# Half-row level scaling in a chunked linear attention, and a 128-row rope product with a bf16 mask in the latent attention

## The chip, the core and the metric

The kernel runs on one core of a Trainium2 chip. The metric is device time in microseconds, measured over whole executions; the medians below come from separate runs. In the rows, PE is the matrix engine, PEld its weight load, DVE the vector engine, ACT the scalar engine, POOL the GpSimd engine and SP the engine that issues most DMAs.

## What is computed

The kernel computes two transformer blocks on 512 tokens with a model width of 1024: a layer with gated linear attention (4 heads, key width 128, value width 256), a SwiGLU layer, a layer with latent attention (8 heads, 128 plain and 64 rotated key columns), a SwiGLU layer, then a block with a pooling and a convolution branch, and an expert layer with 16384 experts. Only two places matter here.

The linear attention, within one chunk (the reference takes 64 positions, the kernel 128, which is the same sum):

```python
b = jnp.cumsum(gi, axis=-2)
diff = b[:, :, :, None, :] - b[:, :, None, :, :]
decay = jnp.exp(jnp.where(causal, diff, -jnp.inf))
attn = jnp.einsum('bhik,bhjk,bhijk->bhij', qi, ki, decay)
o_intra = jnp.einsum('bhij,bhjv->bhiv', attn, vi)
```

The latent attention, for a block of 128 queries:

```python
s = (jnp.einsum('bqhd,bkhd->bhqk', qn_b, k_nope)
     + jnp.einsum('bqhd,bkd->bhqk', qr_b, k_rope)).astype(jnp.float32) * scale
p = jax.nn.softmax(jnp.where(mask, s, -jnp.inf), axis=-1)
return jnp.einsum('bhqk,bkhd->bqhd', p.astype(v.dtype), v)
```

## The kernel before

Each engine has its own instruction stream, written out by hand; `wait_ge` and `then_inc` on semaphores tie them together. Nothing reorders the work: what stands behind a waiting instruction on its engine waits too. Activations lie with features on the partitions and the 512 tokens along the free dimension. Large weights arrive as 128x1024 blocks in a ring of four buffers; ACT rounds a block to `w_hi`, POOL subtracts to get `w_lo` (L551), and PE makes three products for each pair (`unit`), all recorded at L1626, the line of the helper `mm`.

**The linear attention.** The decayed product of a chunk of 128 positions is built from 7 levels and a diagonal. At level `l` the chunk is cut into blocks of `2s` with `s = 128 >> (l + 1)`; queries in the second half of a block meet keys in its first half, both scaled by `exp(-|b - b_ref|/16)` with the reference position in the middle. An item is one head and one level (or the diagonal), 4 x 8 = 32 items. For an item DVE subtracts the reference (`gate_sums`, L1211), ACT takes the absolute value and the exponential in place (L693, L694, two buffers `g_E`), DVE scales queries and keys (`scaled`, L1219 and L1220, two buffers each), PE multiplies in four chunks of 128 columns into one of four banks of `pa` (`items`), and DVE copies what the level's mask keeps into `g_attn` (`keep`, L1228). DVE's order in turn n is: gate sums of the next item, scaling of item n, mask copy of item n-1. PE does items 0 to 17 in pairs between the projection blocks of `v` and `r`, and items 18 to 31 one after the other behind the twelfth block. Two more blocks of `r` follow on PE, while ACT and DVE scale `g_q` and `g_k` for the state's products, for which PE then waits.

**The latent attention.** 8 heads times 4 query blocks make 32 steps. In step s PE computes the scores of query block `s % 4` against 128, 256, 384 or 512 keys, and after them the transposes of step s-2 (1 to 4 of 128 columns, L1905); once per head it adds the 8 records of the product with `v`. The scores are three products that accumulate in one bank: `m_kn` with `m_qn` (128 rows), `m_kr` with `m_qr` (64 rows: even heads in partitions 0 to 63, odd heads in 64 to 127) and an fp32 product of the identity with the causal mask for the last 128 columns. DVE takes the maximum (L1384) and its negative (L1385), ACT the exponential with its sum (L857), and DVE, in step s+1 behind the maximum of that step, the reciprocal (L1389) and the scaling (L1391), on which the transposes wait. ACT copies the transposes out (L864). The rotated key `m_kr` is made once before that (L1367 to L1369), and ACT waits for it (`kr_done`) before it reads the rotated queries' products into the same buffers (L830).

Of the kernel before, what the change touches and what calls it, by code (L numbers as in the profile page):

```python
# [24 lines left out]
BF16 = mybir.dt.bfloat16  # L25
# [123 lines left out]
def two_blocks(nc, A, out):  # L149
# [59 lines left out]
    g_E = ar("g_E", 56 * K, [2, S])  # L209
    g_qs = ar("g_qs", 60 * K, [2, S])  # L210
    g_ks = ar("g_ks", 64 * K, [2, S])
    g_ln = ar("g_ln", 56 * K, [GH, S])
# [25 lines left out]
    m_v = ar("m_v", 40 * K, [TT, MH * MVD])  # L238
    m_kr = ar("m_kr", 56 * K, [S])
    m_cos = ar("m_cos", 58 * K, [S])  # L240
# [11 lines left out]
    c_hi = at("c_hi", ada_off, [5, S], F32R)  # L252
    m_st = at("m_st", ada_off + 10 * K, [MH * TT, 4])

    ssq = ar("ssq", 0, [DT, S])
# [517 lines left out]
    def act_mla(act, hi):  # L773
# [42 lines left out]
        for t in range(12):  # L816
# [4 lines left out]
            if t < MH:  # L821
                nc.scalar.activation(m_qn[:, t, :], bank, ACT.Copy).then_inc(tile_free, 1)
            else:
                j = t - MH
                act.wait_ge(kr_done, 1)
                if j >= 2:
                    act.wait_ge(qr_done, j - 1)
                dst = (m_sw, m_kraw)[j % 2]
                for q in range(4):
                    nc.scalar.activation(dst[32 * q:32 * q + 32, :], bank[32 * (q ^ 1):32 * (q ^ 1) + 32, :], ACT.Copy)\  # L830
                      .then_inc(sw_done, 1)
# [327 lines left out]
    def dve_gla(dve):  # L1159
# [42 lines left out]
        def gate_sums(e):  # L1202
# [8 lines left out]
            nc.vector.tensor_tensor(E, b, ref, ALU.subtract).then_inc(lv_d, 1)  # L1211

        def scaled(n):

            h, l, e = item_level(n)
            dve.wait_ge(lv_e, e + 1)
            if e >= 2:
                dve.wait_ge(lv_mm, (e - 2) // LEVELS * (LEVELS + 1) + (e - 2) % LEVELS + 1)
            nc.vector.tensor_tensor(g_qs[:, e % 2, :], g_q[:, h, :], g_E[:, e % 2, :], ALU.mult)  # L1219
            nc.vector.tensor_tensor(g_ks[:, e % 2, :], g_k[:, h, :], g_E[:, e % 2, :], ALU.mult).then_inc(lv_q, 1)  # L1220

        def keep(n):
# [3 lines left out]
            if n:  # L1226
                dve.wait_ge(lv_cp, n)
            nc.vector.copy_predicated(g_attn[:, h, :].rearrange("p (c i) -> p c i", c=TT), bc(g_mask[:, l, :], 1, TT),  # L1228
                                      pa[:, n % 4, :].rearrange("p (c i) -> p c i", c=TT)).then_inc(lv_cp, 1)

# [103 lines left out]
    def dve_mla(dve):  # L1334
# [31 lines left out]
        dve.wait_ge(tile_free, T0["mla_qn"])  # L1366
        step(v.tensor_tensor(m_kr[:, :], m_kraw[:, :], m_cos[:, :], ALU.mult))  # L1367
        step(v.tensor_tensor(m_sw[:, :], m_sw[:, :], m_sin[:, :], ALU.mult))
        v.tensor_tensor(m_kr[:, :], m_kr[:, :], m_sw[:, :], ALU.add).then_inc(kr_done, 1)  # L1369
        T = T0["mla_qr"]  # L1370
# [338 lines left out]
    def pe_gla(pe):  # L1709
# [11 lines left out]
        def items(n):  # L1721

            while taken[0] < n:
# [8 lines left out]
                for c in range(TT):  # L1732
                    w = slice(c * GCH, (c + 1) * GCH)
                    kk, qq = (g_ks[:, e % 2, w], g_qs[:, e % 2, w]) if l < LEVELS else (g_k[:, h, w], g_q[:, h, w])
                    last = mm(pa[:, a % 4, w], kk, qq, True, True)
# [103 lines left out]
    def pe_mla(pe):  # L1839
# [46 lines left out]
        pe.wait_ge(qr_done, MH // 2)  # L1886
        pe.wait_ge(kr_done, 1)
        n_it = MH * TT
        for s in range(n_it + 3):
            if s < n_it:  # L1890
# [3 lines left out]
                n, q = P * (qb + 1), slice(qb * P, (qb + 1) * P)  # L1894
                half = slice(ROPE * (h % 2), ROPE * (h % 2 + 1))
                mm(pa[:, s % 3, 0:n], m_qn[:, h, q], m_kn[:, h, 0:n], True, False)
                mm(pa[:, s % 3, 0:n], m_qr[half, h // 2, q], m_kr[half, 0:n], False, False)
                mm(pa[:, s % 3, n - P:n], ident, const("causal_t", P), False, True).then_inc(at_s, 1)
            if 2 <= s < n_it + 2:
# [267 lines left out]
```

## Time and profile before

| | |
|---|---|
| median of 3 runs | 3224.52 us (3216.39 to 3231.88) |
| profiled execution | 3218.98 us, its span 3217.1 us |
| mean granted TensorE clock | 0.983 of full speed |
| PE / DVE / ACT / POOL busy | 96% / 50% / 36% / 55% |
| linear attention, items behind the last projection block | 189.7 to 225.5 us |
| latent attention, score steps | 806.8 to 902 us |

Busy time of PE is the time in which a matmul was in flight, so that it can be near 100% while the array is not at its peak. An fp32 matmul stands as two records, and each streams its columns twice; an fp32r matmul stands as one. The span is cut at the first and last instruction.

### The profile page before, as it was taken

The numbers are of one execution on the slowest core, as the hardware profiler recorded it, in microseconds if no ns is written. First come the engines' busy times: TensorE is split into PE (matmuls) and PEld (weight loads), VectorE is DVE, ScalarE is ACT, GpSimd is POOL, SyncE is SP. The second block draws the span as 40 slices with busy tenths as digits, with TensorE's granted clock in tenths as the row PEclk, the third lists the DMA queues.
The fourth block names the chain that finished last, engine by engine and source line by source line (L and its number), as shares of the span: only waits on it lengthen the run. The fifth ranks groups of instructions, "written<-read, shape, count | busy, mean of one in ns | idle before, by whom it ended". The sixth has DMA issues, their size and how long they took to land.

```text
span 3217.1 us, 44185 instructions
## 1 busy us (share of the span) xinstructions
PE 3085.6 (96%) x14632; PEld 2500.8 (78%) x14632; DVE 1608.6 (50%) x2785; ACT 1151.3 (36%) x1478; POOL 1775.1 (55%) x2040
## 2 busy tenths in 40 slices
PE   5988999998999999997999999999999999999998
PEld 3777788876568888775788888888888888888887
DVE  7873455322435552595316997444421444544443
ACT  4354322226342223433333234555543332333332
POOL 4833677645037766673545665444445666666663
PEclk8989999999999999998999999999999999999999
DMA  7511455522015554221323444555555655556552
GB/s 307 208 35 57 145 200 176 167 77 90 7 61 199 199 172 133 89 84 54 104 92 98 151 147 144 196 187 194 193 198 190 209 192 182 180 195 209 201 190 78
DMA packets 170201, 481.94 MB, mean 150 GB/s; under 512 B 15360, under 2 KB 48896, under 8 KB 168080
## 3 DMA queue, kind: packets, MB, share of 16 engines
q1 hardware_dynamic: 147680, 410.83, 39.1%
q10 hardware_dynamic: 22448, 70.14, 5.6%
q8 instruction: 46, 0.75, 0.1%
q14 instruction: 27, 0.22, 0.0%
HBM read 411.70 MB, written 69.21 MB: 149 GB/s over the span
## 4 chain that ended last, share of the span: by engine, by line
PE 52%; issue 23%; POOL 21%; DVE 2%; ACT 0%; DMA 0%; DVEq 0%; POOLq 0%; SPq 0%; ACTq 0%
PE ps L1626 49%; POOL w_lo L551 21%; PE pa L1626 4%; DVE s_acc L1420 1%; DMA e_g<-expert_act 0%; DVEq L1417 0%; DVE s_pb L1432 0%; DVE s_tmp L1471 0%; DVE mg_lo L1473 0%; ACT mg_hi L921 0%; DVE s_m L1469 0%; DVE x L1125 0%; POOLq L549 0%; POOLq L555 0%; DVE s_gl L1412 0%
## 5 line engine op out<-in xcount | busy, mean ns | idle before, releaser
L551 POOL TENSOR_TENSOR w_lo<-raw,w_hi 128x256 fp32r<-128x256 f32 x2036 | 1774.9, 903 | 1412.6 <-ACT w_hi L569 1411.3
L1626 PE MATMUL ps<-h_hi,w_hi 128*128 128x512 f32 x2392 | 944.8, 395 | 33.4 <-POOL w_lo L551 22.8
L1626 PE MATMUL ps<-h_hi,w_lo 128*128 128x512 f32 x2392 | 934.2, 391 | 0.0
L1626 PE MATMUL ps<-h_lo,w_hi 128*128 128x512 f32 x2392 | 914.5, 390 | 0.0
L569 ACT ACTIVATE w_hi<-raw 128x1024 fp32r<-128x1024 f32 x509 | 538.6, 1060 | 803.9 <-PE ps L1626 685.5
L1626 PEld LDWEIGHTS ps<-h_hi,w_hi 128*128 128x128 f32 x2392 | 450.6, 188 | 133.7 <-POOL w_lo L551 24.5
L1626 PEld LDWEIGHTS ps<-h_hi,w_lo 128*128 128x128 f32 x2392 | 450.6, 188 | 95.5
L1626 PEld LDWEIGHTS ps<-h_lo,w_hi 128*128 128x128 f32 x2392 | 450.4, 188 | 93.0 <-issue 1.7
L1626 PE MATMUL ps<-wa_hi,w_hi 128*128 128x512 f32 x1024 | 398.5, 389 | 0.5 <-DVE x L1590 0.5
L1626 PE MATMUL ps<-wa_hi,w_lo 128*128 128x512 f32 x1024 | 398.4, 389 | 0.0
L1626 PE MATMUL ps<-wa_lo,w_hi 128*128 128x512 f32 x1024 | 398.3, 389 | 0.0
L1072 DVE CUSTOM_DVE_ANT_0 ada<-ada,cvec 128x1024 f32<-128x1024 f32 x144 | 229.3, 1630 | 34.9 <-DMA ada<-in_ada 30.7
L1626 PEld LDWEIGHTS ps<-wa_hi,w_hi 128*128 128x128 f32 x1024 | 192.3, 188 | 40.8 <-DVE x L1590 0.9
L1626 PEld LDWEIGHTS ps<-wa_hi,w_lo 128*128 128x128 f32 x1024 | 192.3, 188 | 39.9
L1626 PEld LDWEIGHTS ps<-wa_lo,w_hi 128*128 128x128 f32 x1024 | 192.3, 188 | 39.8
L1583 DVE TENSOR_TENSOR wa_lo<-e_t,wa_hi 128x512 fp32r<-128x512 f32 x128 | 137.4, 1074 | 153.8 <-ACT wa_hi L1008 153.8
L928 ACT ACTIVATE g_act<-ps 128x512 f32<-128x512 f32 x128 | 76.5, 598 | 348.1 <-PE ps L1626 348.1
L1580 DVE TENSOR_TENSOR e_t<-e_g,e_w 128x512 f32<-128x512 f32 x128 | 110.4, 863 | 168.1 <-DMA e_g<-expert_act 167.3
L1590 DVE SCALAR_TENSOR_TENSOR x<-ps,mod,x 128x512 f32<-128x512 f32 x128 | 95.5, 746 | 158.5 <-PE ps L1626 158.3
L1008 ACT ACTIVATE wa_hi<-e_t 128x512 fp32r<-128x512 f32 x128 | 80.8, 631 | 222.6 <-DVE e_t L1580 222.6
L1555 DVE TENSOR_TENSOR oh_hit<-iota_t,r_key 128x1024 bf16<-128x1024 bf16 x64 | 45.9, 718 | 213.5 <-PE pa L1626 213.1
L988 ACT ACTIVATE w_st<-pa 128x512 f32<-128x512 f32 x128 | 134.7, 1167 | 39.3 <-PE pa L1626 39.3
(315 smaller groups left out, 3104.7 us busy)
## 6 DMA issues: line engine op xcount, KB each, us to landing
ada<-in_ada SPq DMA_DIRECT2D x144, 512.0 KB, 4.4
raw<-in_expert_u SPq DMA_DIRECT2D x128, 512.0 KB, 4.1
raw<-in_expert_v SPq DMA_DIRECT2D x128, 512.0 KB, 4.2
raw<-in_ffn_in SPq DMA_DIRECT2D x88, 512.0 KB, 3.5
expert_act<-g_act ACTq DMA_DIRECT2D x128, 256.0 KB, 4.2
gate_matrix<-w_st ACTq DMA_DIRECT2D x16, 2048.0 KB, 6.9
e_w<-gate_matrix SPq DMA_DIRECT2D x16, 2048.0 KB, 11.4
e_g<-expert_act SPq DMA_DIRECT2D x128, 256.0 KB, 7.5
```

The lines of the kernel that those rows point to most:

```text
L551: last = nc.gpsimd.tensor_tensor(w_lo[:, k, c:c + 256], raw[:, k, c:c + 256], w_hi[:, k, c:c + 256].bitcast(F32), ALU.subtract)
L569: nc.scalar.activation(w_hi[:, k, :], raw[:, k, :], ACT.Copy).then_inc(hi_done, 1)
L928: nc.scalar.activation(g_act[:, k % 2, :], ps[:, (T + k) % RING, :], ACT.Gelu_apprx_tanh)\
L988: nc.scalar.activation(w_st[:, b, :, 4 * q:4 * q + 4].rearrange("p n t -> p t n"), pa[:, q % 4, :].rearrange("p (t n) -> p t n", t=4), ACT ...
L1008: nc.scalar.activation(wa_hi[:, b, k, :], e_t[:, :], ACT.Copy).then_inc(wa_h, 1)
L1072: return nc.vector.tensor_tensor_reduce(out=w, in0=w, in1=cvec[:, :], scale=1.0, scalar=0.0, op0=ALU.mult, op1=ALU.add, accum_out=dst).the ...
L1420: v.scalar_tensor_tensor(out=s_acc[:, t, :], in0=s_gl[:, t, bass.ds(i + 1, S)], scalar=cols[:, bass.ds(i + (COLS["dw_kernel"] + t * CK + 1 ...
L1555: v.tensor_tensor(oh_hit[:, b, :, :, :], column, key1, ALU.is_equal).then_inc(oh_hits, 1)
L1580: v.tensor_tensor(e_t[:, :].rearrange("p (t k) -> p t k", k=WTOK), e_g[:, k % 4, :].rearrange("p (t k) -> p t k", k=WTOK), e_w[:, :, k, :] ...
L1583: v.tensor_tensor(wa_lo[:, b, k, :], e_t[:, :], wa_hi[:, b, k, :].bitcast(F32), ALU.subtract).then_inc(wa_done, 1)
L1590: v.scalar_tensor_tensor(out=x[:, k, :], in0=ps[:, (T + k) % RING, :], scalar=mod[:, GATE[6] + k:GATE[6] + k + 1], in1=x[:, k, :], op0=ALU ...
L1626: return nc.tensor.matmul(out, a, b, start=start, stop=stop_)
```

## The change

In the linear attention the two scaled copies `g_qs` and `g_ks` become one tile `g_kq` with four buffers in place of two: the first half of each block of `2s` columns gets the scaled keys, the second half the scaled queries. PE reads it as both operands. The mask copy of a level reads and writes only the columns of second halves, which are the only ones that its mask can keep; the diagonal is copied in full as before. In the latent attention the rotated key stands in two tiles, each with zeros in the 64 partitions of the other parity, so that the rope product uses all 128 rows with both heads' queries; identity and mask are held in bf16 too. The first loads and the convolution are the same as before.

```diff
-    g_qs = ar("g_qs", 60 * K, [2, S])
-    g_ks = ar("g_ks", 64 * K, [2, S])
+    g_kq = ar("g_kq", 60 * K, [4, S])
...
-    m_kr = ar("m_kr", 56 * K, [S])
+    m_kr = [ar("m_kr0", 56 * K, [S]), at("m_kr1", rstd_off, [S])]
...
-                act.wait_ge(kr_done, 1)
+                act.wait_ge(kr_done, 6)
...
+        def halves(row, l, half):
+
+            s = GCH >> (l + 1)
+            return row.rearrange("p (n w) -> p n w", w=2 * s)[:, :, half * s:(half + 1) * s]
+
         def scaled(n):
 
             h, l, e = item_level(n)
             dve.wait_ge(lv_e, e + 1)
-            if e >= 2:
-                dve.wait_ge(lv_mm, (e - 2) // LEVELS * (LEVELS + 1) + (e - 2) % LEVELS + 1)
-            nc.vector.tensor_tensor(g_qs[:, e % 2, :], g_q[:, h, :], g_E[:, e % 2, :], ALU.mult)
-            nc.vector.tensor_tensor(g_ks[:, e % 2, :], g_k[:, h, :], g_E[:, e % 2, :], ALU.mult).then_inc(lv_q, 1)
+            if e >= 4:
+                dve.wait_ge(lv_mm, (e - 4) // LEVELS * (LEVELS + 1) + (e - 4) % LEVELS + 1)
+            for half, rows in enumerate((g_k, g_q)):
+                last = nc.vector.tensor_tensor(halves(g_kq[:, e % 4, :], l, half), halves(rows[:, h, :], l, half),
+                                               halves(g_E[:, e % 2, :], l, half), ALU.mult)
+            last.then_inc(lv_q, 1)
...
+            s = GCH >> (l + 1)
+            nc.vector.copy_predicated(halves(g_attn[:, h, :], l, 1).rearrange("p (c n) i -> p c n i", c=TT),
+                                      bc(halves(g_mask[:, l, :], l, 1), 1, TT),
+                                      halves(pa[:, n % 4, :], l, 1).rearrange("p (c n) i -> p c n i", c=TT)).then_inc(lv_cp, 1)
...
-                    kk, qq = (g_ks[:, e % 2, w], g_qs[:, e % 2, w]) if l < LEVELS else (g_k[:, h, w], g_q[:, h, w])
+                    kk, qq = (g_kq[:, e % 4, w],) * 2 if l < LEVELS else (g_k[:, h, w], g_q[:, h, w])
...
-        step(v.tensor_tensor(m_kr[:, :], m_kraw[:, :], m_cos[:, :], ALU.mult))
+        step(v.tensor_tensor(m_t[:, :], m_kraw[:, :], m_cos[:, :], ALU.mult))
         step(v.tensor_tensor(m_sw[:, :], m_sw[:, :], m_sin[:, :], ALU.mult))
-        v.tensor_tensor(m_kr[:, :], m_kr[:, :], m_sw[:, :], ALU.add).then_inc(kr_done, 1)
+        for a in range(2):
+            mine, other = slice(ROPE * a, ROPE * (a + 1)), slice(ROPE * (1 - a), ROPE * (2 - a))
+            v.memset(m_kr[a][other, :], 0.0).then_inc(kr_done, 1)
+            v.tensor_tensor(m_kr[a][mine, :], m_t[mine, :], m_sw[mine, :], ALU.add).then_inc(kr_done, 1)
+        v.tensor_copy(ident_b[:, :], ident).then_inc(kr_done, 1)
+        v.tensor_copy(causal_b[:, :], const("causal_t", P)).then_inc(kr_done, 1)
...
-                half = slice(ROPE * (h % 2), ROPE * (h % 2 + 1))
                 mm(pa[:, s % 3, 0:n], m_qn[:, h, q], m_kn[:, h, 0:n], True, False)
-                mm(pa[:, s % 3, 0:n], m_qr[half, h // 2, q], m_kr[half, 0:n], False, False)
-                mm(pa[:, s % 3, n - P:n], ident, const("causal_t", P), False, True).then_inc(at_s, 1)
+                mm(pa[:, s % 3, 0:n], m_qr[:, h // 2, q], m_kr[h % 2][:, 0:n], False, False)
+                mm(pa[:, s % 3, n - P:n], ident_b[:, :], causal_b[:, :], False, True).then_inc(at_s, 1)
```

On DVE, in the level loop (`g_E` are the gate sums, `g_qs` and `g_ks` the scaled copies), before:

```order
L1211 TENSOR_TENSOR g_E<-g_b 128x512
L1219 TENSOR_TENSOR g_qs<-g_q,g_E 128x512
L1220 TENSOR_TENSOR g_ks<-g_k,g_E 128x512
L1228 COPY_PREDICATED g_attn<-g_mask,pa 128x512
L1211 TENSOR_TENSOR g_E<-g_b 128x512
```

And the same engine with the change, two turns (levels 4 and 5; the three sizes are partitions, runs and length of a run):

```order
L1212 TENSOR_TENSOR g_E<-g_b 128x512
L1226 TENSOR_TENSOR g_kq<-g_k,g_E 128x64x4
L1226 TENSOR_TENSOR g_kq<-g_q,g_E 128x64x4
L1241 COPY_PREDICATED g_attn<-g_mask,pa 128x32x8
L1212 TENSOR_TENSOR g_E<-g_b 128x512
L1226 TENSOR_TENSOR g_kq<-g_k,g_E 128x128x2
L1226 TENSOR_TENSOR g_kq<-g_q,g_E 128x128x2
```

The order of a turn is unchanged. Three of its four instructions go from 512 to 256 columns.

On DVE, where the key is rotated, before, with the last steps of the latent norm ahead and the first query tile behind:

```order
L1363 TENSOR_TENSOR c_lo<-m_c,c_hi 128x512 x2
L1367 TENSOR_TENSOR m_kr<-m_kraw,m_cos 128x512
L1368 TENSOR_TENSOR m_sw<-m_sw,m_sin 128x512
L1369 TENSOR_TENSOR m_kr<-m_kr,m_sw 128x512
L1375 TENSOR_TENSOR m_qr<-m_cos,ps 128x512
```

And with the change:

```order
L1381 TENSOR_TENSOR m_t<-m_kraw,m_cos 128x512
L1382 TENSOR_TENSOR m_sw<-m_sw,m_sin 128x512
L1385 MEMSET m_kr_99 64x512
L1386 TENSOR_TENSOR m_kr_99<-m_t,m_sw 64x512
L1385 MEMSET m_kr_100 64x512
L1386 TENSOR_TENSOR m_kr_100<-m_t,m_sw 64x512
L1387 CAST ident_b<-consts 128x128
L1388 CAST causal_b<-consts 128x128
```

One add becomes six instructions, and `kr_done` counts all six. On PE the order of products and transposes is the same as before, with the operands of the diff.

## Rows read from the trace of the kernel before

**Rows 1.** The page, busy time of each engine.

```profile
PE 3085.6 (96%) x14632; PEld 2500.8 (78%) x14632; DVE 1608.6 (50%) x2785; ACT 1151.3 (36%) x1478; POOL 1775.1 (55%) x2040
```

**Rows 2.** Windows: stretch, us, busy of each engine, PEclk, DMA share, GB/s.

```profile
132.10:189.70 57.60, 57.60 (x306) 49.68 (x306) 44.69 (x56) 28.43 (x43) 40.10 (x38) 0.97 0.27 83
189.70:225.50 35.80, 26.23 (x134) 23.36 (x133) 31.85 (x53) 14.48 (x24) 0.00 (x0) 0.71 0.05 15
...
806.80:820.20 13.40, 13.18 (x34) 6.42 (x34) 3.91 (x15) 2.40 (x8) 0.00 (x0) 0.62 0.01 3
820.20:893.00 72.80, 70.63 (x288) 39.36 (x288) 33.35 (x118) 30.19 (x92) 0.00 (x0) 1.00 0.00 1
```

**Rows 3.** Timeline of DVE, one level turn: start, us, line, out<-in.

```profile
210.66 0.68 DVE L1211 TENSOR_TENSOR g_E<-g_b 128x512 f32<-128x512 f32 x1
211.26 0.68 DVE L1219 TENSOR_TENSOR g_qs<-g_q,g_E 128x512 f32<-128x512 f32 x1
211.86 0.69 DVE L1220 TENSOR_TENSOR g_ks<-g_k,g_E 128x512 f32<-128x512 f32 x1
212.47 0.72 DVE L1228 COPY_PREDICATED g_attn<-g_mask,pa 128x512 f32<-128x512 uint32 x1
```

**Rows 4.** Timeline of DVE, first and last mask copy of the exposed turns.

```profile
190.81 0.75 DVE L1228 COPY_PREDICATED g_attn<-g_mask,pa 128x512 f32<-128x512 uint32 x1 [0.66 <-PE pa L1626]
...
224.76 0.73 DVE L1228 COPY_PREDICATED g_attn<-g_mask,pa 128x512 f32<-128x512 uint32 x1 [0.19 <-PE pa L1626]
```

**Rows 5.** Timeline of PE, level products at either granted clock.

```profile
207.87 1.13 PE L1626 MATMUL pa<-g_qs,g_ks 128*128 128x128 f32 x8 [1.02 <-DVE g_ks L1220]
...
219.93 3.86 PE L1626 MATMUL pa<-g_qs,g_ks 128*128 128x128 f32 x16 [1.28 <-DVE g_ks L1220]
```

**Rows 6.** Timeline of PE in attention: start, us, line, out<-in.

```profile
847.60 1.02 PE L1626 MATMUL pa<-m_kn,m_qn 128*128 128x512 f32 x2
848.55 1.12 PE L1626 MATMUL pa<-m_kr,m_qr 64*128 64x512 f32 x2
849.61 0.49 PE L1626 MATMUL pa<-consts 128*128 128x128 f32 x2
849.93 0.38 PE L1905 MATMUL ps<-consts,m_P 128*128 128x128 f32 x2
...
851.59 0.55 PE L1905 MATMUL ps<-consts,m_P 128*128 128x128 f32 x3 [0.23 <-DVE m_P L1391]
```

**Rows 7.** Groups by form, 806 to 902 us: busy, mean ns | idle before.

```profile
L1384 DVE TENSOR_REDUCE m_st<-pa 128x1 f32<-128x512 f32 x8 | 5.5, 692 | 26.4 <-PE pa L1626 26.4
...
L1384 DVE TENSOR_REDUCE m_st<-pa 128x1 f32<-128x256 f32 x8 | 3.4, 425 | 6.6 <-PE pa L1626 6.6
```

**Rows 8.** Timeline of ACT in the turn of rows 3.

```profile
211.38 0.63 ACT L693 ACTIVATE g_E<-g_E 128x512 f32<-128x512 f32 x1 [1.12 <-DVE g_E L1211]
212.04 0.63 ACT L694 ACTIVATE g_E<-g_E 128x512 f32<-128x512 f32 x1
```

**Rows 9.** The page: ACT out of PSUM, output in one run and in strides.

```profile
L928 ACT ACTIVATE g_act<-ps 128x512 f32<-128x512 f32 x128 | 76.5, 598 | 348.1 <-PE ps L1626 348.1
...
L988 ACT ACTIVATE w_st<-pa 128x512 f32<-128x512 f32 x128 | 134.7, 1167 | 39.3 <-PE pa L1626 39.3
```

**Rows 10.** Timeline of DVE, second scaling of the first head.

```profile
129.16 1.21 DVE L1220 TENSOR_TENSOR g_ks<-g_k,g_E 128x512 f32<-128x512 f32 x1
```

**Rows 11.** Timeline of PE around bf16 products of the routing stage.

```profile
2016.28 1.56 PE L1626 MATMUL pa<-oh_gate,oh_key 128*128 128x128 bf16 x24
2017.65 0.47 PE L1626 MATMUL ps<-h_hi,w_hi 128*128 128x512 f32 x1
```

**Rows 12.** Timeline of DVE in attention, scaling of a 512-column tile.

```profile
852.63 0.49 DVE L1391 TENSOR_SCALAR m_P<-m_P,m_st 128x512 f32<-128x512 f32 x1
```

**Rows 13.** Timelines of DVE and ACT around the key rotation.

```profile
760.06 1.11 DVE L1369 TENSOR_TENSOR m_kr<-m_kr,m_sw 128x512 f32<-128x512 f32 x1
...
771.76 2.43 ACT L830 ACTIVATE m_sw<-ps 32x512 f32<-32x512 f32 x4 [2.05 <-PE ps L1626]
```

More of the change, by code:

```diff
@@ L253, in two_blocks @@
     m_st = at("m_st", ada_off + 10 * K, [MH * TT, 4])
+    ident_b = at("ident_b", ada_off + 10 * K + 512, [P], BF16)
+    causal_b = at("causal_b", ada_off + 10 * K + 768, [P], BF16)
     ssq = ar("ssq", 0, [DT, S])
@@ L1227, in keep @@
                 dve.wait_ge(lv_cp, n)
-            nc.vector.copy_predicated(g_attn[:, h, :].rearrange("p (c i) -> p c i", c=TT), bc(g_mask[:, l, :], 1, TT),
-                                      pa[:, n % 4, :].rearrange("p (c i) -> p c i", c=TT)).then_inc(lv_cp, 1)
+            if l == LEVELS:
+                nc.vector.copy_predicated(g_attn[:, h, :].rearrange("p (c i) -> p c i", c=TT), bc(g_mask[:, l, :], 1, TT),
+                                          pa[:, n % 4, :].rearrange("p (c i) -> p c i", c=TT)).then_inc(lv_cp, 1)
+                return
+            s = GCH >> (l + 1)
+            nc.vector.copy_predicated(halves(g_attn[:, h, :], l, 1).rearrange("p (c n) i -> p c n i", c=TT),
+                                      bc(halves(g_mask[:, l, :], l, 1), 1, TT),
+                                      halves(pa[:, n % 4, :], l, 1).rearrange("p (c n) i -> p c n i", c=TT)).then_inc(lv_cp, 1)
         dve.wait_ge(tile_free, T0["gla_v"])
@@ L1886, in pe_mla @@
         pe.wait_ge(qr_done, MH // 2)
-        pe.wait_ge(kr_done, 1)
+        pe.wait_ge(kr_done, 6)
         n_it = MH * TT
```

## The prediction

> **What bounds the kernel now.** I read the page's engine lines first: PE is busy for 96% of the span, the others for at most 55% [rows 1]. So the change pays where PE waits, or where PE's own work gets shorter, and nowhere else. Busy time hides both, since a matmul in flight counts as busy. I therefore cut the two stages into windows and then went to the timelines.
>
> In the linear attention PE has two phases. From 132.1 to 189.7 us it is busy for 57.60 of 57.60 us at a granted clock of 0.97, with projection blocks and pairs of items [rows 2]. There DVE is ahead and waits, and a shorter DVE turn buys nothing. From 189.7 to 225.5 us PE has only items, and is busy for 26.2 of 35.8 us at a clock of 0.71, while DVE is busy for 31.9 [rows 2]. The timeline of DVE shows why: four instructions of 512 columns follow each other 0.60 us apart (210.66, 211.26, 211.86, 212.47), so a turn takes 2.41 us [rows 3]. The first mask copy of this phase starts at 190.81 us and the last at 224.76, 33.95 us for 14 items: 12 levels and 2 diagonals [rows 4]. PE needs 1.13 us for an item at 2.4 GHz, and 3.86 us for two at 1.2 GHz [rows 5], so it is not the bound at either clock. DVE is.
>
> In the latent attention it is PE. From 820.2 to 893 us PE is busy for 70.6 of 72.8 us at full clock, DVE for 33.4, ACT for 30.2 [rows 2]. The reader should look at the starts of the score products. The two records with `m_kn` start at 847.60, the two with `m_kr` at 848.55, the two of the mask at 849.61, the transposes at 849.93 [rows 6]. From first to last that is 2.33 us. The columns alone need less: a record streams its columns twice, so at 2.4 GHz 512 columns take 0.43 us and 128 take 0.11, and four records of the one and two of the other make 1.92. About 0.4 us is left over. It sits around the 64-row product: that group takes 1.06 us, where 0.86 would do, and 0.1 is lost on either side of it. Only once per head does PE wait for somebody: 0.23 us before the transposes at 851.59 [rows 6], or 0.39 counted from where the columns before it end.
>
> **The half rows.** In a turn, two scalings and one mask copy go from 512 to 256 columns; the gate sums stay. No such instruction stands in this trace, so I take the slope from the maximum: 692 ns for 512 columns, 425 for 256 [rows 7], 0.267 us less. A turn becomes 0.60 + 3 x (0.60 - 0.267) = 1.60 us.
>
> Three things could hold it above that. ACT takes 0.63 + 0.63 us for an item, starting about 0.7 us behind the gate sums (211.38 against 210.66) [rows 3, 8]; its result is there 2.0 us after they start. The scaling that needs it stands one gate sum, two scalings, one mask copy and one more gate sum later, 2.2 us. ACT keeps up, by 0.2 us. PE at 2.4 GHz needs about 1.1 us, hidden. PE at 1.2 GHz needs 1.93 us an item, so there PE is the bound and a turn takes 1.9 us. Twelve turns then save 12 x 0.81 = 9.7 us at full clock or 12 x 0.48 = 5.8 us at half clock. The clock was 0.71 here because PE idled between items; with shorter gaps I expect a mixture again and take 7.7. The items at which DVE waits for PE anyway, behind the last level of a head and at the end, gain or lose little.
>
> What follows moves with it: the two `r` blocks on PE start when the last item ends, and the chain of ACT and DVE that scales `g_q` and `g_k` starts when the last mask copy does. POOL is idle in this stretch [rows 2], so the weights for those blocks are ready. At the front of the stage PE waits for the first two items. A scaling takes 1.21 us there, beside POOL [rows 10]; two scalings at half length give 0.7 to 1.2 us, less what the mixture with ACT keeps. I take 0.8. The interleaved phase itself gives nothing, since PE does the same records in it. Four buffers for two remove a wait that costs nothing now. Sum for this stage: 8.5 us, between 5 and 11.5.
>
> The half rows have runs of 64 down to 1 column at a distance of twice that. Nearest to them in this trace is an instruction of another engine: ACT writes 512 columns in 598 ns in one run, and in 1167 ns where the output goes out in strides [rows 9]. If the half rows of DVE paid that factor, each would cost as much as a full row does now, and the stage would give nothing but noise. The Trainium skill ("Advanced Engine Details and Errata", Memory Cachelines) says that SBUF works at full rate if at least two accesses fall on one 16-byte line, and that PSUM has lines of 8 bytes. By that rule all levels' SBUF accesses stay at full rate, since a stride of two fp32 columns still puts two on a line, the strided write of ACT does not, and only the mask copy of the last level, which reads every other column of PSUM, could be slower. By the rule the loss is 0.27 us for each of the two such copies in the exposed phase; by the ACT row it is 8 us.
>
> **The rope product.** Its columns cost the same with 128 rows as with 64: `m_kn` shows it. What goes is the 0.4 us around it. The mask goes from two fp32 records, 0.22 us, to one bf16 record. Bf16 products run 24 in 1.37 us (2016.28 to 2017.65), 0.057 us each, and the fp32r product behind them is 0.08 us longer than its like, 0.47 against 0.39, because its weights take longer than one short record [rows 11]. I count 0.11 us for the mask with what follows, so 0.11 saved. Each step saves 0.39 + 0.11 = 0.50 us of PE, 2.0 us per head.
>
> Not all of it arrives. The transposes at 851.59 wait for a chain: end of the 512-column scores at 850.10 (849.61 + 0.49), maximum, negative, reciprocal, scaling, 1.5 us. In that time PE does two transposes and the scores of 128 columns. They get 0.5 us shorter, and PE just waits 0.9 us where it waited 0.39. Behind it, the four transposes of the next step need the scaling of 512 columns, which ends 1.53 us after 851.59 (852.63 + 0.49) [rows 6, 12]. PE comes there after three transposes (0.33), four records of 256 columns (0.87) and the mask (0.11), at 1.3 to 1.4 us. So it waits 0.2 us. Of 2.0 us per head 0.5 and 0.2 are lost, and some 0.05 comes back from the shorter mask ahead of the maximum: 1.34 us. The waits at 820.20 and 893.44 are seven heads apart, 7 x 1.34 = 9.4 us. The first head runs at a clock of 0.62 [rows 2], where gaps and mask cost more; four steps give about 2.6 us. The last steps are a chain of DVE and ACT, unchanged. Sum: 12 us, between 8 and 13.5.
>
> **The new work on DVE.** The key's rotation ended at 761.17 us (760.06 + 1.11). It gets two memsets and one more add of 512 columns and two casts of 128. None can cost more than the 1.11 us of the add beside POOL: five times 1.11 is 5.6 us, so `kr_done` is full by 766.8. ACT asks for it at 771.76, when it has waited 2.05 us for PE [rows 13]. Cost nothing, with 5 us to spare; without that cover it would be at most 5.6.
>
> **Sum.** 3218.98 - 8.5 - 12.0 = 3198.5 us for the profiled execution. That one lies 5.5 us under the median of the runs shown, so against the median it is 3224.5 - 20.5 = 3204 us.
>
> **Rivals.**
> - *Half rows at full price* (12%). Short runs cost DVE what the strided output costs ACT [rows 9]. Against it: it is another engine, and its strides are far wider, 32 columns for 2 to 128 here. Only the 12 us of the attention stay: 3212.
> - *The gap is not the 64 rows* (12%). What the timeline shows is that the weights of the `m_kr` product, and of the next one, don't load under the product before. If any change of form does that, the bf16 mask between fp32 products brings the 0.2 us back on both sides. The bf16 rows speak against it: going in costs nothing that I can see [rows 11]. The attention then gives the mask's 0.1 us a step and little more, 3 us: 3213.
> - *The clock falls in the attention* (6%). This is the case that ends slower. PE now waits 1.1 us of a head's 9.1, twice a head; where it idled between items the granted clock was 0.71 [rows 2]. A head needs some 7.7 us of columns at 2.4 GHz and twice that at 1.2. With half the stage at 1.2 GHz, four heads lose 6 to 7 us each, 26 us, against 20.5 gained: 3230. It turns into a loss from about three heads on. Against it: the array itself idles less than before, when 1.6 us of gaps and 0.39 of waiting stood in 10.5.
>
> **How the numbers follow.** The forecast has 70%; its own range is 3198 to 3210, from 13 to 25 us saved and 2 us of spread. The first two rivals reach to 3213, and with the spread of the runs (7 us on either side of the median) I give 3192 to 3217. What a measurement can tell from no change is 0.5%, 16 us, or 3208.4. The forecast lies below that in about 9 of 10 of its cases, the first two rivals above it nearly always. So faster 64%, same 30%, slower 6%.
>
> **What would show it.** Right: the mask copies of the exposed phase span 25 to 27 us for 33.95; DVE's half rows take about 0.41 to 0.47 us; score products in attention start with no gap, the `m_kr` group 0.86 us long at 512 columns; the period from wait to wait is 9.1 us for 10.46, and the wait before the short step's transposes is near 0.7 to 0.9 us. Wrong: half rows of 0.7 us; weight loads of the mask that start only after the rope product; a granted clock under 0.95 between the attention's second and last head.

## Result and the profile after

The changed kernel took 3190.1 us, the median of 4 runs (3189.6 to 3190.3). Four runs of the kernel before beside it gave 3228.2 us (3216.4 to 3234.1); the ratio is 0.9886, 95% interval [0.9856, 0.9916]. The profiled executions stand at 3189.6 and 3218.98 us, 29.4 apart. In 60 more runs beside the experiments the kernel before had a median of 3220.5 us, so 29 to 30 us, 0.9%, is the fair size of the gain. Forecast were 20.5 us and 3204 us, with a range of 3192 to 3217. The time fell below the range, by 2 us.

The page, busy time of each engine, answers to [rows 1]:

```profile
PE 3056.9 (96%) x14600; PEld 2488.8 (78%) x14600; DVE 1592.6 (50%) x2790; ACT 1151.4 (36%) x1478; POOL 1769.3 (56%) x2040
```

The windows of the same stages, as in [rows 2]: interleaved phase, exposed phase, first head, next seven heads, last steps.

```profile
131.00:188.70 57.70, 57.70 (x308) 49.73 (x307) 37.37 (x56) 29.62 (x45) 33.60 (x38) 0.98 0.30 88
188.70:213.60 24.90, 17.84 (x132) 15.76 (x132) 22.14 (x52) 14.46 (x23) 0.00 (x0) 1.00 0.06 20
791.20:803.00 11.80, 10.02 (x43) 6.88 (x44) 5.72 (x22) 5.13 (x17) 0.00 (x0) 0.86 0.10 37
803.00:864.20 61.20, 54.66 (x248) 33.53 (x247) 31.95 (x111) 28.91 (x86) 0.00 (x0) 1.00 0.00 1
864.20:874.00 9.80, 7.06 (x30) 5.03 (x31) 1.75 (x4) 3.10 (x7) 2.82 (x4) 1.00 0.17 54
```

The number behind the five engines' columns is the granted clock. It was 0.71 in the exposed phase and 0.62 in the first head [rows 2]; it is 1.00 and 0.86 here.

The timeline of DVE answers to [rows 3, 4]: the first mask copy of the exposed phase, the copies of the last two levels of one head, a turn with long runs, the last two copies.

```profile
189.60 0.45 DVE L1241 COPY_PREDICATED g_attn<-g_mask,pa 128x256 f32<-128x256 uint32 x1 [1.77 <-PE pa L1645]
...
197.63 0.72 DVE L1241 COPY_PREDICATED g_attn<-g_mask,pa 128x256 f32<-128x256 uint32 x1
199.02 0.73 DVE L1241 COPY_PREDICATED g_attn<-g_mask,pa 128x256 f32<-128x256 uint32 x1 [0.67 <-PE pa L1645]
...
203.07 0.68 DVE L1212 TENSOR_TENSOR g_E<-g_b 128x512 f32<-128x512 f32 x1
203.67 0.41 DVE L1226 TENSOR_TENSOR g_kq<-g_k,g_E 128x256 f32<-128x256 f32 x1
204.01 0.41 DVE L1226 TENSOR_TENSOR g_kq<-g_q,g_E 128x256 f32<-128x256 f32 x1
204.34 0.42 DVE L1241 COPY_PREDICATED g_attn<-g_mask,pa 128x256 f32<-128x256 uint32 x1
204.68 0.68 DVE L1212 TENSOR_TENSOR g_E<-g_b 128x512 f32<-128x512 f32 x1
...
211.99 0.73 DVE L1241 COPY_PREDICATED g_attn<-g_mask,pa 128x256 f32<-128x256 uint32 x1 [0.68 <-PE pa L1645]
212.89 0.73 DVE L1237 COPY_PREDICATED g_attn<-g_mask,pa 128x512 f32<-128x512 uint32 x1 [0.17 <-PE pa L1645]
```

A turn takes 204.68 - 203.07 = 1.61 us, forecast 1.60. The copies span 23.3 us (189.60 to 212.89) for 33.95, less than the 25 to 27 foreseen. In the kernel before, DVE waited longer for PE ahead of the last level's copy of each head:

```profile
205.22 0.73 DVE L1228 COPY_PREDICATED g_attn<-g_mask,pa 128x512 f32<-128x512 uint32 x1 [1.59 <-PE pa L1626]
...
223.83 0.74 DVE L1228 COPY_PREDICATED g_attn<-g_mask,pa 128x512 f32<-128x512 uint32 x1 [1.46 <-PE pa L1626]
```

These two waits are 0.67 and 0.68 us here (199.02, 211.99), 1.7 us less in all.

The timeline of PE in the attention answers to [rows 6]:

```profile
833.34 1.02 PE L1645 MATMUL pa<-m_kn,m_qn 128*128 128x512 f32 x2
834.20 1.02 PE L1645 MATMUL pa<-m_kr,m_qr 128*128 128x512 f32 x2
835.06 0.22 PE L1645 MATMUL pa<-causal_b,ident_b 128*128 128x128 bf16 x1
835.11 0.39 PE L1923 MATMUL ps<-consts,m_P 128*128 128x128 f32 x2
...
836.77 0.55 PE L1923 MATMUL ps<-consts,m_P 128*128 128x128 f32 x3 [0.77 <-DVE m_P L1410]
```

From `m_kn` to the transposes it is 1.77 us where it was 2.33. The same wait follows at 845.90 (836.77 + 9.13).

Where the 29.4 us of the profiles are, by the starts of the same instructions in both traces:

| place | saved, us | forecast |
|---|---|---|
| front of the level loop | 1.2 | 0.8 |
| exposed phase, first to last mask copy | 10.7 | 7.7 |
| first attention head, first product to first wait of a short step's transposes (13.42 to 8.21) | 5.2 | 2.6 |
| seven heads, wait to wait (73.24 to 63.74) | 9.5 | 9.4 |
| last steps of the attention | 1.7 | 0 |
| all the rest | 1.1 | 0 |

The last row is 2.7 us between level loop and attention less 1.6 behind it; in 17 profiles those stretches vary by 4 and 10 us whatever the change, so I take it for noise. The last steps differ in one group, the last head's product with `v`: 4.12 us for its 8 records before (timeline, 895.97), 2.42 after (866.70). The record of the granted clock has half clock there. So the parts that depend on columns, gaps and waits came out as forecast, and the missing part lies where the granted clock differs. Theory A: that clock belongs to the change. Rival B: it was an accident of one profile.

### The profile page after: what moved, and what is told of

Read it like the earlier page. It is cut to its first block, busy times and chain, and to the rows that moved or that the text cites. A ratio compares the mean times of both kernels' runs of the same rounds, so it can differ in the third digit from the quotient of the medians.

```text
span 3187.7 us, 44124 instructions
## 1 busy us (share of the span) xinstructions
PE 3056.9 (96%) x14600; PEld 2488.8 (78%) x14600; DVE 1592.6 (50%) x2790; ACT 1151.4 (36%) x1478; POOL 1769.3 (56%) x2040
## 4 chain that ended last, share of the span: by engine, by line
PE 53%; issue 22%; POOL 21%; DVE 2%; ACT 0%; DMA 0%; DVEq 0%; POOLq 0%; SPq 0%; ACTq 0%
PE ps L1645 49%; POOL w_lo L552 21%; PE pa L1645 4%; DVE s_acc L1439 1%; DMA e_g<-expert_act 0%; DVEq L1436 0%; DVE s_pb L1451 0%; DVE s_tmp L1490 0%; DVE mg_lo L1492 0%; ACT mg_hi L922 0%; DVE s_m L1488 0%; DVE x L1126 0%; POOLq L550 0%; POOLq L556 0%; DVE s_gl L1431 0%
## 5 line engine op out<-in xcount | busy, mean ns | idle before, releaser
L1645 PEld LDWEIGHTS ps<-h_hi,w_hi 128*128 128x128 f32 x2392 | 452.4, 189 | 135.1 <-POOL w_lo L552 23.9
```

The lines of the kernel that those rows point to most:

```text
L1645: return nc.tensor.matmul(out, a, b, start=start, stop=stop_)
```

## The experiments

**The parts alone.** The half rows without the attention's change; the 128-row rope product with the fp32 mask; the bf16 mask with the 64-row product; both attention parts. The edits are the pieces of the diff ahead of the prediction; the middle two wait for `kr_done` of 4 and 3.

> The half rows alone, the latent attention as before. The full change profiled 29.4 us under the profile of before, 20.5 were forecast. Its trace puts 11.9 us of that ahead of the end of the linear attention's level loop (forecast 8.5), 5.2 into the first attention head (forecast 2.6), 9.2 into the next seven (forecast 9.4), 1.7 into the last steps (forecast 0), and the rest into weight waits. Theory A (each part brings its own idle time and its own clock): here the mask copies of the exposed phase span 23.3 us at full granted clock, as with the full change; the first head takes 13.4 us again with a half-clock stretch near 10 us, since its products are as before; 3206 to 3210 us, 11 to 14 us under before. Theory B (the low clock of the first head in the one profile of before was an accident of that run): the first head is at full clock in about half of the profiles, whatever its products.

> The 128-row rope product alone, with the fp32 mask and the full-row level scaling. If the gap of 0.39 us a step sits around the 64-row product: the period from wait to wait is 10.46 - 7 heads' share of it, which is 0.39 x 4 = 1.56 less the 0.5 that the short step's wait takes back, so 9.4 to 9.6 us, the m_kr group of 512 columns takes 1.02 us, and the attention saves 9 to 13 us. If the gap comes from the alternation of products and mask (my rival): the period stays at 10.3 or more. Theory A: the first head at 10 us or less with a short low-clock stretch. Theory B: 13 us or 9, as it falls.

> The bf16 mask alone, with the 64-row rope product and the full-row level scaling. Forecast: 0.11 us a step, 0.4 a head, 3 us in all, period 10.0 to 10.1 us. Rival (the mask's shorter record makes the weight load behind it stand free, between fp32 products): period 10.46 as before or longer.

> Both attention parts, full-row level scaling. Period 9.13 us as with the full change. Exposed phase of the linear attention 34 us with half-clock stretches in it, as before. Theory A: first head near 8.2 us, attention 15 to 16 us shorter in all; 3203 to 3208 us. Theory B: first head between 8 and 11 us. With the half rows' own result the two should add up to the full change, 38 us by the medians of this chip or 29 by the profiles.

| kernel | median us | ratio to before, 95% | period of a head | half clock at the attention's start, us |
|---|---|---|---|---|
| half rows | 3209.4 | 0.9964 [0.9950, 0.9978] | 10.47 | 23.9 |
| rope product | 3211.3 | 0.9969 [0.9957, 0.9980] | 9.45 | 3.4 |
| bf16 mask | 3215.2 | 0.9980 [0.9968, 0.9992] | 9.73 | 17.1 |
| rope and mask | 3201.0 | 0.9937 [0.9920, 0.9954] | 9.13 | 3.4 |

Half rows and attention add up: 0.9964 x 0.9937 = 0.9901 for 0.9886. The half rows and the rope product came out as expected in time; the mask saved 8.1 us by the medians, where 3 were expected, and both attention parts together ran 2 us under the range of 3203 to 3208. The half rows' profile had 23.9 us of half clock at the attention's start, where about 10 were expected. The last column is read from the trace's record of the granted clock. The rope product alone, timeline of PE:

```profile
845.36 1.02 PE L1629 MATMUL pa<-m_kn,m_qn 128*128 128x512 f32 x2
846.22 1.02 PE L1629 MATMUL pa<-m_kr,m_qr 128*128 128x512 f32 x2
847.07 0.39 PE L1629 MATMUL pa<-consts 128*128 128x128 f32 x2
847.29 0.38 PE L1907 MATMUL ps<-consts,m_P 128*128 128x128 f32 x2
```

And the bf16 mask alone:

```profile
835.87 1.02 PE L1630 MATMUL pa<-m_kn,m_qn 128*128 128x512 f32 x2
836.83 1.12 PE L1630 MATMUL pa<-m_kr,m_qr 64*128 64x512 f32 x2
837.88 0.23 PE L1630 MATMUL pa<-causal_b,ident_b 128*128 128x128 bf16 x1
837.95 0.39 PE L1909 MATMUL ps<-consts,m_P 128*128 128x128 f32 x2
```

With 128 rows a step is 0.40 us shorter (1.93 for 2.33), on both sides of the product, so the gap does come from the 64 rows. With the bf16 mask it is 0.25 us shorter (2.08 for 2.33), where I had 0.11: mask and transposes follow each other in 0.07 us, and no weight load shows behind the short record. Together it is 0.56, and the waits take back what they were said to.

**A row of the clock at the attention's start.** Each line is the 27.3 us from the first product, of another kernel; the number ahead of the DMA share is the granted clock. First the kernel before, then once more the kernel before (second profile), then the changed one.

```profile
806.78:834.08 27.30, 26.85 (x91) 14.31 (x92) 10.63 (x39) 8.84 (x29) 0.00 (x0) 0.81 0.01 2
```

```profile
801.86:829.16 27.30, 27.30 (x64) 14.15 (x65) 6.93 (x26) 6.25 (x20) 0.00 (x0) 0.56 0.01 2
```

```profile
792.21:819.51 27.30, 24.88 (x110) 16.08 (x111) 14.11 (x51) 11.70 (x37) 0.00 (x0) 0.94 0.01 2
```

> The kernel before once more, unchanged, for a second profile of it. In 39 runs of it so far the time follows the granted clock: 3181 us plus 0.35 us for each us at half clock, with 96 to 142 us at half clock. If the 64-row products draw the half-clock stretch of the first head out by a varying length, it is anywhere from 10 to 30 us here, with 5.4 us lost for a whole head at half clock; if the one profile of before was typical, 10.2 us again.

The second profile had 23.9 us of half clock there, and its second head took 16.0 us for 10.46, from its first product to that of the next head (814.29 to 830.30). It ran 3230 us. So B is half right: the length varies from run to run. But it varies in one kind of kernel only. Over the 60 runs of before, time is 3180 us plus 0.36 us for each us at half clock (correlation 0.90), with 96 to 142 us of it in a run (twice the span times what the run's mean clock lacks to 1). The changed kernel has 77 in all four runs, which lie within 0.7 us of each other; before, the lowest and the highest run lie 17 us apart.

**Rows or gaps?** The 64-row product has fewer rows and gaps around it. Three kernels separate these, the first two of them profiled twice. In the changed kernel PE waits for itself ahead of the rope product and behind it (gaps, 128 rows):

```diff
-                mm(pa[:, s % 3, 0:n], m_qn[:, h, q], m_kn[:, h, 0:n], True, False)
-                mm(pa[:, s % 3, 0:n], m_qr[:, h // 2, q], m_kr[h % 2][:, 0:n], False, False)
+                mm(pa[:, s % 3, 0:n], m_qn[:, h, q], m_kn[:, h, 0:n], True, False).then_inc(own_pe, 1)
+                pe.wait_ge(own_pe, 2 * s + 1)
+                mm(pa[:, s % 3, 0:n], m_qr[:, h // 2, q], m_kr[h % 2][:, 0:n], False, False).then_inc(own_pe, 1)
+                pe.wait_ge(own_pe, 2 * s + 2)
```

In the changed kernel the first head alone takes 64 rows (`rows = slice(0, ROPE if h == 0 else P)`); in the kernel before the first head alone takes 128.

> The changed kernel, but in the attention PE waits for the end of its own product ahead of the 128-row rope product and again behind it, so that PE has gaps there as it had around the 64-row product, with all 128 rows in use. With 64-row products the first head's half-clock stretch was 10.2, 17.1 and 23.9 us long in three profiles, with 128 rows 3.4 us in three. If the gaps do that: the stretch is 10 us or more here too, a second one stands at the end of the attention (896 us in before, none in the changed kernel), and the runs spread over 10 us and more. If the number of rows does it: the stretch stays 3.4 us, and the runs within 3 us. In either case the period of a head is longer than 9.13 us by the gaps, 32 waits of 0.1 to 0.3 us on either side: 9.9 to 11 us, and the total 3197 to 3210.

> The changed kernel with gaps around the 128-row rope product, for a second profile. Rows decide it: 3.4 us of half clock at the attention's start again. Gaps do it too: 10 us or more in this one.

> The changed kernel, but in the first head alone, four steps, the rope product takes the 64 rows that hold the key, with the same tiles. The gaps cost 0.39 us a step, 1.6 us. If the 64-row products draw out the low clock at the attention's start: a half-clock stretch of 7 us or more there, the first head 3 to 6 us longer than the 13.9 us of the changed kernel, runs spread over 3 us or more, 3193 to 3197. If they don't: 3.4 us of half clock as in all six profiles with 128 rows, 15.5 us for the first head, 3191 to 3192.

> The changed kernel with 64 rows in the first head's rope product, for a second profile. Rows decide it: 10 us or more of half clock at the attention's start again. The stretch of 10.2 us at the attention's end, where all products have 128 rows, comes back if it belongs to this kernel, and is gone if it was a chance.

> The kernel before with 128 rows in the rope product of the first head alone; the other 28 steps take 64 rows, the mask is fp32, the level scaling full. Five profiles with 64 rows in the first head had half-clock stretches of 10.2 to 23.9 us at the attention's start, eight with 128 rows 3.4 us. If the rows decide it: 3.4 us here, the first head 14 to 15 us from its first product to its evacuation in place of 20 to 26, a period of 10.46 us in the other heads. If it hangs on the density of the whole stage: 10 us or more. The total 5 to 8 us under before.

| profiles | rows in the first head | gaps | half clock at the start, us |
|---|---|---|---|
| before (2), half rows, bf16 mask, products twice | 64 | yes | 10.2, 23.9, 23.9, 17.1, 10.2 |
| 64 rows in the first head (2) | 64 | yes, 4 steps | 13.7, 13.7 |
| 128 rows, waiting for itself (2) | 128 | yes, larger | 3.4, 6.8 |
| 128 rows in the first head of before | 128 | not in its 4 steps | 3.4 |
| the other seven with 128 rows | 128 | no | 3.4 each |

One clock row for each of three, from the first product: 64 rows in the first head, waiting for itself (first profile), 128 rows in the first head of before.

```profile
793.55:820.85 27.30, 26.31 (x89) 14.29 (x90) 11.82 (x43) 9.87 (x32) 0.00 (x0) 0.75 0.01 3
```

```profile
791.53:818.83 27.30, 25.61 (x91) 12.25 (x92) 11.78 (x43) 10.01 (x32) 0.00 (x0) 0.94 0.01 3
```

```profile
806.49:833.79 27.30, 26.85 (x107) 15.99 (x107) 11.77 (x43) 10.62 (x33) 0.00 (x0) 0.94 0.01 3
```

The reader should set the PE column against the clock: 26.31 us busy at 0.75, 25.61 at 0.94. Four products of 64 rows in the first 11 us make the difference: 10 us of half clock and 5.0 us of time (18.98 us from the first product until ACT copies out the head's product with `v`, 13.93 in the changed kernel). Of these 5.0 us the gaps are 1.6 by an estimate, 4 x 0.40. The added rows hold zeros in the key, and the stretch is short with them all the same.

The kernel that waits for itself didn't settle gaps as cleanly: the rows alone were to give 3.4 us and runs within 3 us, the gaps 10 us and runs spread over 10. It had 3.4 us at the start in one profile and 6.8 in the other, and its eight runs spread over 8.6 us. So rows decide the long stretch, and gaps may add to the rest.

By medians, 64 rows in the first head take 3199.8 us, ratio to before 0.9933 [0.9910, 0.9957], against 3190.1 for the changed kernel, above the 3193 to 3197 expected. The two intervals touch, and the nearest kernel measured beside it, the one with full-row copies below, had 3193.0 us, so the difference is 7 to 10 us. The kernel that waits for itself takes 3208.1, 0.9971 [0.9960, 0.9982], with a period of 10.65 us. The reverse, 128 rows in the first head of the kernel before, had that head in 15.4 us (14 to 15 expected) for 20.1, and 3215.9 us, ratio 0.9986 [0.9971, 1.0001]. That is 5.0 us under the median beside it, at the lower end of the 5 to 8 expected, and not settled as a time, since the interval takes in no change. The end of the attention isn't explained: half clock stands there for 3.4 to 6.8 us in the kernels with 64-row products, for 10.2 in both profiles with 64 rows in the first head alone, where these are 70 us back, and for 10.2 and 3.4 in those that wait for themselves, but not in the other seven.

**The exposed phase.** Products of items 18 to 31 twice, in the kernel before; and in the changed kernel a maximum over 512 columns ahead of the scalings, to lengthen DVE's turn.

```diff
-                for c in range(TT):
+                for c in [c for c in range(TT) for _ in range(2 if a >= 18 else 1)]:
...
+            if n >= 18:
+                nc.vector.tensor_reduce(g_x[:, n - 18:n - 17], g_b[:, h, :], AX.X, ALU.max)
```

> The kernel before, but PE makes the products of items 18 to 31 twice into the same bank. If idle PE between items costs the clock: granted clock 1.00 in the exposed phase (0.71 before), DVE the bound with turns of 2.41 us, mask copies spanning 31 to 33 us, the total 0 to 3 us under before. If the clock falls for another reason: half-clock stretches of 20 us in the phase stay, and since PE needs 3.9 us for a doubled item there, the phase grows to 40 us or more.

> The changed kernel, but from item 18 on DVE takes a maximum over 512 columns ahead of the scalings, which nothing uses. A turn goes from 1.60 to 2.2 us, the exposed phase from 23.3 to 30.5 us, the total to 3197. If idle PE between items costs the clock: half-clock stretches of 7 to 17 us come back in the exposed phase, as in the four kernels with turns of 2.41 us. If the halved operands or the single tile for both operands of the product do it: none.

Windows of the phase, first the doubled products, then the longer turns:

```profile
189.30:225.90 36.60, 30.35 (x245) 28.40 (x245) 31.89 (x53) 14.54 (x24) 0.00 (x0) 1.00 0.05 15
```

```profile
189.00:221.40 32.40, 20.85 (x133) 18.54 (x132) 29.14 (x64) 14.45 (x23) 0.00 (x0) 0.89 0.04 16
```

PE that works 30 of 36.6 us keeps full clock, and PE that idles more than in the changed kernel loses it for 6.8 us, just under the 7 to 17 expected. The other profiles agree: six with turns of 2.41 us and single products have 13.7 to 20.5 us of half clock in the phase, the one with turns of 2.2 us has 6.8, and of eight with turns of 1.6 us six have none and two (half rows alone, full-row copies) have 3.4. Theory A holds: the clock there goes with PE's idle time between items. The longer turns took 30.6 us from first to last copy, as expected, and 3200.5 us, 3.5 above.

What the clock was worth to the kernel before, the doubled products can't say: a doubled product at full clock takes PE 2.02 us, as long as a single one at half clock (2.05). Its copies took 34.8 us (31 to 33 expected) and its time was the same, 3221.0 (ratio 1.0001 [0.9988, 1.0013]). The other profiles say it. With single products DVE's turn is 2.41 us at either clock, but the wait ahead of the last level's copy is 1.59 us at half clock and 0.67 at full, so that from first to last copy it was 33.95 us in the profile shown, and about 32.1 in that of the rope product alone, where both waits were 0.67. So the clock was worth up to 1.9 us there. In the changed kernel half clock also makes PE the bound of a turn: with 3.4 us of it the copies took 24.0 and 24.1 us for 23.3.

**Mask copies of the last two levels over the full row** (`if l >= LEVELS - 2:` for `if l == LEVELS:`).

> The changed kernel, but the mask copies of the last two levels (runs of 2 columns, and single columns) cover the full row as before. In the changed kernel these copies of 256 columns took 0.72 and 0.73 us, those of the levels with longer runs 0.41 to 0.45 us, and the full row of the diagonal 0.73 us. If a strided copy out of PSUM is what is slow, the full row costs the same: copies of 0.73 us, exposed phase 23.3 us, no difference in time (within 0.5 us). If the copies were slow for another reason, such as waiting for the product: 0.73 us plus that, 0.3 us each, 1.2 us in the exposed phase.

Timeline of DVE, the copies of levels 4 to 6 and the diagonal:

```profile
198.23 0.42 DVE L1241 COPY_PREDICATED g_attn<-g_mask,pa 128x256 f32<-128x256 uint32 x1
199.83 0.73 DVE L1237 COPY_PREDICATED g_attn<-g_mask,pa 128x512 f32<-128x512 uint32 x1
201.22 0.74 DVE L1237 COPY_PREDICATED g_attn<-g_mask,pa 128x512 f32<-128x512 uint32 x1 [0.66 <-PE pa L1645]
203.12 0.74 DVE L1237 COPY_PREDICATED g_attn<-g_mask,pa 128x512 f32<-128x512 uint32 x1
```

A half row in runs of one or two columns costs what a full row costs. The median was 3193.0 us, 2.9 above the changed kernel, where a difference within 0.5 was expected. The copies have equal durations and so don't explain it; the profile has 3.4 us of half clock in the phase that the changed kernel's hasn't, and what else differs stays open.

**Two versions that go on.** The product with `v` stands one step later (`if s >= 7 and (s - 7) % TT == 0:` on PE and ACT, 8 on DVE). On top of it, three items behind each block, and a mask copy two turns late:

```diff
-        return 0 if b < 3 else min(ITEMS, (b - 2) * 2)
+        return 0 if b < 3 else min(ITEMS, (b - 3) * 3 + 2)
...
-            if n:
-                keep(n - 1)
+            if n >= 2:
+                keep(n - 2)
+        keep(ITEMS - 2)
```

> The changed kernel, but the product with v of a head stands one step later on PE, behind the 512-column scores and the transposes of the next head's second step, with its readers on ACT and DVE one step later too. There PE waits 0.77 us for the scaling ahead of the short step's transposes and 0.11 to 0.26 ahead of the next, while DVE and ACT work off the 512-column scores. The 2.2 us of the product should cover both waits: the period of a head goes from 9.13 to 8.0 to 8.2 us, seven heads save 7 to 8 us, 3182 to 3184. Rival: the wait goes elsewhere, since without the product ahead of them the transposes of the second step wait for their scaling instead; then 0 to 4 us.

> The kernel with the later v product, and more items between the projection blocks: PE does three in place of two behind each block from the second on, 26 in place of 18 by the last, and DVE copies the product of item n-2 in turn n in place of n-1. With pairs DVE waited 2.0 to 3.8 us for PE in each period of 7.24 us; a third turn of 1.6 us (2.4 us beside POOL) fits into 8.1 us. PE's items behind the last block go from 14 to 6: the phase from the last block's item to the last product goes from 22.5 to about 9.5 us, the blocks' phase grows by 8 items of 0.87 us, 7 us, net 6 us: 3177. The rival: beside POOL a turn takes 3.4 us, PE waits for the third item in most periods, and the gain shrinks to 0 to 3 us.

The first gave 3183.3 us, ratio to before 0.9887 [0.9870, 0.9903]; the period is 7.95 us for 9.13, and no wait is left before the transposes of the short step (819.60 below). Its timeline of PE:

```profile
816.71 0.39 PE L1923 MATMUL ps<-consts,m_P 128*128 128x128 f32 x2
816.94 2.32 PE L1645 MATMUL ps<-m_PT,m_v 128*128 128x512 f32 x8
819.09 0.39 PE L1645 MATMUL pa<-m_kn,m_qn 128*128 128x128 f32 x2
819.32 0.39 PE L1645 MATMUL pa<-m_kr,m_qr 128*128 128x128 f32 x2
819.54 0.22 PE L1645 MATMUL pa<-causal_b,ident_b 128*128 128x128 bf16 x1
819.60 0.50 PE L1923 MATMUL ps<-consts,m_P 128*128 128x128 f32 x3
```

The second gave 3175.4 us, 0.9850 [0.9823, 0.9876]. Its windows of the interleaved phase and of the six items left behind the last block:

```profile
131.00:188.00 57.00, 57.00 (x328) 50.01 (x327) 46.23 (x77) 34.09 (x52) 31.55 (x34) 0.98 0.28 87
188.00:207.00 19.00, 16.88 (x113) 14.95 (x112) 15.21 (x32) 9.47 (x16) 3.78 (x4) 1.00 0.10 29
```

PE stays full in the first, and DVE has room left (46.2 of 57). The rival, waits for the third item, didn't come.

## Why the prediction was right and where it was wrong

- *What bounds the two stages.* Right. DVE in the exposed phase, PE in the attention.
- *The turn, 1.60 us.* Right, 1.61. ACT and PE kept up as said, but for one wait of 0.35 us for ACT in the last head.
- *"The clock was 0.71 here because PE idled between items; with shorter gaps I expect a mixture again and take 7.7."* **The term that failed in the linear attention.** The cause was right (both exposed-phase runs show it), the size wrong: the clock stayed at 1.00, and the phase saved 10.7 us, 1.0 us more than even my full-clock end of 9.7. I took for half the phase a clock that the shorter gaps did away with.
- *"The items at which DVE waits for PE anyway ... gain or lose little."* **The second term that failed there**, and why 9.7 wasn't the end. The two waits ahead of the last level's copies were 1.59 and 1.46 us at half clock before and are 0.67 and 0.68: 1.7 us. Against it, ten copies became cheaper and not the 12 that I counted. From 190.81 to 224.76 us DVE makes 16 copies, 14 of levels and 2 of diagonals (the 14 items that I named are PE's), and four of the 14 cost a full row's time.
- *"The first head runs at a clock of 0.62, where gaps and mask cost more; four steps give about 2.6 us."* **The step that failed in the attention.** I took the clock of 0.62 as given and priced only the shorter work in it. The runs show that the 64-row products themselves draw the half clock out: 10.2 to 23.9 us of it with them in seven profiles, 3.4 without in nine of ten and 6.8 in one. So the first head gave 5.2 us against the profile shown, and 6 us more than that against the second profile (26.09 us until ACT's first copy-out for 20.09).
- *"The last steps are a chain of DVE and ACT, unchanged."* Wrong by 1.7 us, one product at half clock before. I put the gain there at nothing by looking at the waits alone. What sets the clock there stays open.
- *The period, 9.1 for 10.46 us; the wait of 0.7 to 0.9.* Right: 9.13 and 0.77. Inside it the mask was undersized: on top of the 128-row product it gives 0.16 us a step (0.56 - 0.40) for 0.11.
- *The rope's work on DVE costs nothing.* Right: the second cast ends at 750.5 us, and ACT, which asks for it at 757.2, has waited 2.05 us for PE.
- *Half rows at full price.* Didn't happen, but for the mask copies of two levels of seven. The copies of single columns took 0.73 us and those of runs of two columns 0.72, both the price of a full row; with longer runs they took 0.41 to 0.45 us. The Trainium skill ("Advanced Engine Details and Errata", Memory Cachelines) gives PSUM lines of 8 bytes, two fp32 values, from which I had single columns alone as slower. The trace agrees for these, and not for runs of two. The measurement decides. That it is the read out of PSUM that is slow, no run isolates: the scalings out of SBUF with the same strides took 0.41 to 0.43 us.
- *The gap is not the 64 rows.* Refuted by the rope product alone.
- *The clock falls in the attention.* It didn't, and the first head went the other way: full rows raised it. PE was busy for 54.7 of 61.2 us in the next seven heads, a smaller share than before (70.6 of 72.8), and the clock stayed at 1.00.
- *The base.* 3204 was set against a median of three runs that lay 4 us above the median of 60. Against 3220.5 my sum gives 3200, 10 us above the result. The terms named are 3.4 (11.9 for 8.5 in the linear attention), 2.6 and 1.7 us, 7.7 in all. The other 2 us I put down to the untouched stretches and to the longer half clock in most runs of before; no run separates them.

## What to carry to other kernels

Where a row shows a granted clock below 1, ask what in the change could raise it, and price the stage at full clock as one end of the range: here the three places where the clock differed gave 7.7 of 29.4 us more than was forecast. By an estimate from the runs of before, 14 of 30 us went with the clock (39 us less at half clock, at 0.36), though 77 us of half clock lie outside the 96 to 142 from which the 0.36 comes. The work removed came out as counted. A product that uses half the rows can cost more than its columns and gaps: in the first head four of them went with 13.7 us of half clock for 3.4, while the engine showed as busy. And when a turn becomes shorter, look at once for the schedule that was cut to the long one: three items for two, and a product moved into a wait, gave 15 us more.

## What the runs showed that I had not expected

- Half clock at a stage's start lasts 10.2 to 23.9 us with 64-row products and 3.4 to 6.8 with 128-row ones, at nearly equal busy time of PE. In the second profile of before PE was busy for 27.30 of 27.30 us at a clock of 0.56, so a full busy time doesn't mean full clock. The Trainium skill ("TensorE: Matmul & The Clock Gate", Part 1) says that the default is the low clock and that activity releases it. The changed kernel agrees: the clock fell at the first score product, behind a wait of 2.15 us, and rose again 3.4 us later under dense products.
- Most of the spread between runs of the kernel before goes with half-clock time (correlation 0.90). The spread is 17 us from the lowest to the highest of 60 runs, and 0.7 us in four of the changed kernel.
- A predicated copy out of PSUM of 256 columns takes 0.41 to 0.45 us in runs of 4 columns and more, 0.72 in runs of 2 and 0.73 in single columns, as much as 512 columns in one run (0.73). Multiplications out of SBUF with the same strides take 0.41 to 0.43.
